# One decoder layer on one core: TensorE for the conditioning rows, tokens on partitions in the tail, other places for small loads

## The reference, cut to what matters

```python
c_act = silu(c)
sh1, sc1, gt1, sh2, sc2, gt2 = split(c_act @ ada_w + ada_b, 6)
h = rmsnorm(x, norm_mix_g) * (1 + sc1) + sh1
x = x + gt1 * hybrid_mixer(h)             # mixer ends in y @ w_out
h = rmsnorm(x, norm_ffn_g) * (1 + sc2) + sh2
logits = h @ router_w + router_b          # top 4 of 32, softmax over the 4
x = x + gt2 * moe(h, logits)              # act(h @ w1[e] + b1[e]) @ w2[e] + b2[e]
out = rmsnorm(x, final_norm_g)
```

## Time and profile before

| | us |
|---|---|
| median of three executions | 1461.37 (1460.83 to 1462.33) |
| the profiled execution | 1460.91 |
| its span, first to last instruction | 1459.1 |
| mean granted TensorE clock, share of full | 0.971 |

### The profile page before, as it was taken

How to read it: one execution, slowest core, us unless ns; L and a number is a source line. 1 busy time by engine, 2 the same in 40 slices (tenths; PEclk the granted TensorE clock), 3 DMA queues, 4 the chain that set the end, 5 groups by cost and what they waited for, 6 DMA issues and landing times.

```text
span 1459.1 us, 17602 instructions
## 1 busy us (share of the span) xinstructions
PE 1324.6 (91%) x6612; PEld 674.9 (46%) x6613; DVE 426.0 (29%) x1020; ACT 175.1 (12%) x355; POOL 73.8 (5%) x67
## 2 busy tenths in 40 slices
PE   1799998898998799999999999999999999989996
PEld 1688866878887433333322333233333233323332
DVE  5588625454312421121112111121211121112112
ACT  1000111121200211011001100010110010001102
POOL 1010003324100000000000000000000000000000
PEclk8799989999999799999999999999999999999999
DMA  9968551010434099999999999969999999999995
GB/s 319 387 235 299 192 200 59 0 59 1 141 144 155 27 429 426 426 425 428 427 425 425 428 427 427 424 266 425 428 427 426 425 428 426 427 425 425 429 426 217
DMA packets 68390, 471.79 MB, mean 323 GB/s; under 512 B 3965, under 2 KB 4154, under 8 KB 35466
## 3 DMA queue, kind: packets, MB, share of 16 engines
q1 hardware_dynamic: 67328, 468.89, 78.2%
q0 software_dynamic: 560, 1.40, 0.5%
q10 hardware_dynamic: 474, 1.11, 0.2%
HBM read 470.33 MB, written 1.05 MB: 323 GB/s over the span
## 4 chain that ended last, share of the span: by engine, by line
PE 53%; DMA 40%; DVE 5%; ACT 1%; issue 1%; ACTq 0%; SPq 0%; DVEq 0%
DMA ring<-in_exp_w_dram 39%; PE bank L683 18%; PE bank L1045 16%; PE bank L1071 5%; PE bank L1016 2%; PE bank L888 2%; PE bank L1083 1%; PE bank L885 1%; PE bank L878 1%; DVE region_z L1186 1%; PE bank L1037 1%; PE bank L801 1%; PE bank L705 1%; DMA ring<-in_ada_w_dram 1%; DMA work<-in_gdn_norm_g_dram 1%
## 5 line engine op out<-in xcount | busy, mean ns | idle before, releaser
L1045 PE MATMUL bank<-ring,work 128*64 128x512 f32 x2112 | 472.3, 598 | 48.8 <-DMA ring<-in_exp_w_dram 48.7
L1045 PEld LDWEIGHTS bank<-ring,work 128*64 128x64 f32 x2112 | 144.9, 137 | 372.5 <-issue 272.8
L1071 PE MATMUL bank<-ring,work 128*64 128x512 f32 x1056 | 233.9, 595 | 0.0
L683 PE MATMUL bank<-region_h,ring 128*128 128x256 f32 x832 | 187.4, 387 | 5.8 <-DVE region_h L1203 4.2
L683 PEld LDWEIGHTS bank<-region_h,ring 128*128 128x128 f32 x832 | 160.0, 194 | 29.4 <-DVE region_h L1203 4.3
L1071 PEld LDWEIGHTS bank<-ring,work 128*64 128x64 f32 x1056 | 72.9, 137 | 137.4 <-issue 137.4
L1515 DVE TENSOR_SCALAR work<-bank 128x256 f32<-128x256 f32 x66 | 27.6, 419 | 347.8 <-PE bank L1045 347.8
L642 ACT ACTIVATE work<-work 128x256 f32<-128x256 f32 x66 | 27.5, 416 | 765.2 <-DVE work L1515 765.2
L1542 DVE TENSOR_TENSOR work<-bank,work 128x512 f32<-128x512 f32 x33 | 22.8, 692 | 315.7 <-PE bank L1071 315.7
L1016 PE MATMUL bank<-qkv,work 128*64 128x512 f32 x272 | 65.7, 604 | 2.1 <-ACT qkv L618 2.1
L1083 PE MATMUL bank<-work 64*128 64x512 f32 x264 | 65.6, 615 | 0.8 <-DVE work L1542 0.8
(11 more groups left out here) (269 smaller groups left out, 958.4 us busy)
## 6 DMA issues: line engine op xcount, KB each, us to landing
ring<-in_exp_w_dram SPq DMA_DIRECT2D x192, 2048.0 KB, 23.7
ring<-in_w_in_dram SPq DMA_DIRECT2D x13, 2048.0 KB, 12.0
ring<-in_ada_w_dram SPq DMA_DIRECT2D x12, 2048.0 KB, 12.9
ring<-in_w_gdn_out_dram SPq DMA_DIRECT2D x2, 2048.0 KB, 7.8
ring<-in_w_out_dram SPq DMA_DIRECT2D x2, 2048.0 KB, 7.9
ring<-in_w_pool_out_dram SPq DMA_DIRECT2D x1, 2048.0 KB, 8.9
consts<-in_const_dram SPq DMA_DIRECT2D x1, 1153.0 KB, 6.4
region_x<-in_x_dram SPq DMA_DIRECT2D x2, 512.0 KB, 11.0
```

The source lines that it names most:

```text
L683: mm = nc.tensor.matmul(out_ap, w(k) if w else w_slot(n, j, k), rhs[:, k, :], start=(k == 0), stop=(k == kc - 1))
L1045: mm = nc.tensor.matmul(bank[b][h * SLOTS:(h + 1) * SLOTS, :], xT[:, c % 4, c // 4, :], slot_as(q, 2)[:, i, lo:lo + 512], start=False, sto ...
L1071: mm = nc.tensor.matmul(bank[2][o * SLOTS:(o + 1) * SLOTS, :], actT[:, b, c, h, :], slot_as(4 + b, 2)[:, h, lo:lo + 512], start=(b + h + c ...
```

## The change

**Start.** The `ada` chunks are cut by rows, two 128-row parts of all 2048 columns each. `ada_rows` multiplies them on PE: a column of `c_act`, spread over 32 columns, is stationary, and 512 columns of weights stream; four such calls go to four 32-partition strips of bank 5. ACT copies the bank to `ada_row`, four small matmuls bring it onto partitions (bank 4), and DVE adds the bias. `c` is turned by itself, the constants are loaded in two parts, SP waits for no rows, `hT` signals after each block, and the first projection waits block by block. POOL's small loads wait for `vec_hT`.

**Middle.** After the z pairs, PE computes sh2 @ router_w (g = 0), and spreads gt1 over partitions (g = 1, ACT copies it to `gt1_row`). DVE folds scale2 into `rw` and the product into `rb`.

**Tail.** w_out is streamed against stationary tokens (`mix_out`), so the result has tokens on partitions. DVE multiplies by `gt1_row` and adds x, per 512 columns. The raw x is turned and scored, the norm's factor is applied to the logits, and `h2` is made by DVE (scale) and POOL or DVE (shift) from spread rows. The two halves of the tokens run one behind the other. The mask comes from one comparison for all four ranks and one sum. The expert biases and `final_norm_g` are loaded by SP. Buffers move: the routing tables `b8` to `region_z`, others as named.

```diff
-        chunks = [("ada", cut(ada_w, CW * i)) for i in range(4)]
+        chunks = [("ada", ada_w[0, 2 * P * q:2 * P * (q + 1), 0:2 * D].rearrange("(c p) n -> p c n", p=P))
+                  for q in range(4)]
...
-            sp.dma_start(rows[ROW_C:ROW_C + 8, :], c.rearrange("b (r n) -> (b r) n", n=P)).then_inc(rows_in, 16)
-            sp.dma_start(rows[ROW_ADA_B:ROW_ADA_B + 48, :],
-                         ada_b.rearrange("l (r n) -> (l r) n", n=P)).then_inc(rows_in, 16)
-            sp.dma_start(consts[:, :], const).then_inc(const_in, 16)
+            sp.dma_start(rows[ROW_C:ROW_C + 8, :], c.rearrange("b (r n) -> (b r) n", n=P)).then_inc(c_in, 16)
+            sp.dma_start(consts[:, 0:2 * P], const[:, 0:2 * P]).then_inc(const_in, 16)
             for t in range(T):
                 sp.dma_start(xt[:, t, :], x[0, t * P:(t + 1) * P, :]).then_inc(x_in, 16)
-            sp.wait_ge(rows_in, 16 * 10)
             for n, (kind, src) in enumerate(chunks):
...
+                    dst = slot_as(n % RING, parts_of[kind])
                 sp.dma_start(dst, src).then_inc(landed[n % RING], 16)
+                if n == RING - 1:
+                    sp.dma_start(consts[:, 2 * P:CONST_W], const[:, 2 * P:CONST_W]).then_inc(tables_in, 16)
...
+            sp.wait_ge(vec_x1, 4)
+            for i in range(2):
+                at = slice(i * SLOTS, i * SLOTS + E)
+                sp.dma_start(b1_rows[at, :], exp_b1[0][:, i * D:(i + 1) * D]).then_inc(b_in, 16)
+                sp.dma_start(b2_rows[at, :], exp_b2[0][:, i * 512:(i + 1) * 512]).then_inc(b_in, 16)
+            sp.dma_start(fin_g, final_norm_g.partition_broadcast(P)).then_inc(fin_in, 16)
             sp.wait_ge(vec_route, 1)
...
+            pool.wait_ge(vec_hT, 1)
             pool.dma_start(pw, pool_w[0].rearrange("g p n -> p g n")).then_inc(early_in, 16)
...
+            pool.wait_ge(act_spread, 4)
+            pool.wait_ge(vec_h2, 1)
+            nc.gpsimd.tensor_tensor(h2[:, 0, :], h2[:, 0, :], shift_row, ALU.add).then_inc(pool_h2, 1)
...
-            act.wait_ge(vec_cols, 1)
-            nc.scalar.activation(c_act[:, :], cols[:, ROW_C:ROW_C + 8], ACT.Silu).then_inc(act_c, 1)
+            act.wait_ge(pe_c, 1)
+            nc.scalar.activation(c_act[:, :], bank[7][:, 0:8], ACT.Silu).then_inc(act_c, 1)
...
+            act.wait_ge(used[3], 1)
+            nc.scalar.activation(ada_row, bank[5][:, :], ACT.Copy).then_inc(act_adarow, 1)
...
+                if g:
+                    for i in range(2):
+                        act.wait_ge(pe_gt1, i + 1)
+                        nc.scalar.activation(gt1_row[:, i * 512:(i + 1) * 512], bank[6][:, :],
+                                             ACT.Copy).then_inc(act_gt1, 1)
...
+            for i, row in enumerate((scale_row, shift_row)):
+                act.wait_ge(pe_spread, i + 1)
+                for h in range(2):
...
+                    nc.scalar.activation(row.rearrange("q (c p) -> q p c", c=KC)[:, at, :],
+                                         bank[4 + 2 * i + h][:, :].rearrange("q (p c) -> q p c", c=KC),
+                                         ACT.Copy).then_inc(act_spread, 1)
...
+                    if each:
+                        pe.wait_ge(each, k + 1)
...
+            def ada_rows(q):
+
+                arrived(q)
+                w = slot_as(q % RING, 2)
+                for i in range(2):
+                    for j in range(4):
+                        mm = nc.tensor.matmul(bank[5][32 * j:32 * j + 32, :],
+                                              c_act[:, 2 * q + i:2 * q + i + 1].to_broadcast([P, 32]),
+                                              w[:, i, CW * j:CW * (j + 1)],
+                                              start=(q + i == 0), stop=(q == 3 and i == 1))
+                mm.then_inc(used[q % RING], 1)
+
             pe.wait_ge(const_in, 16)
-            pe.wait_ge(rows_in, 16 * 10)
+            pe.wait_ge(c_in, 16)
+            nc.tensor.transpose(bank[7][:, 0:8], rows[ROW_C:ROW_C + 8, :], ident[0:8, 0:8]).then_inc(pe_c, 1)
+            pe.wait_ge(act_c, 1)
+            ada_rows(0)
+            pe.wait_ge(vec_xn, 2)
+            for f in range(KC):
+                for t in range(T):
+                    mm = nc.tensor.transpose(turned(f)[:, t * P:(t + 1) * P], xt[:, t, f * P:(f + 1) * P], ident)
+            mm.then_inc(pe_xT, 1)
+            ada_rows(1)
+            ada_rows(2)
+            pe.wait_ge(rows_in, 16 * 9)
...
+            ada_rows(3)
+            pe.wait_ge(act_adarow, 1)
+            for i in range(4):
+                mm = nc.tensor.matmul(bank[4][:, 4 * i:4 * i + 4], ada_row[:, i * P:(i + 1) * P],
+                                      ident.rearrange("p (j a) -> p a j", j=4)[:, 0, :], start=True, stop=True)
+            mm.then_inc(pe_adacol, 1)
...
+
+            def spread(cols_, half, b):
+
+                for j in range(4):
+                    f = 4 * half + j
+                    mm = nc.tensor.matmul(bank[b][:, j * P:(j + 1) * P], cols_[:, f:f + 1].to_broadcast([P, P]), ident,
+                                          start=True, stop=True)
+                return mm
...
+                if g == 0:
+                    for k in range(KC):
+                        mm = nc.tensor.matmul(bank[6][:, 0:E], mod[:, 24 + k:25 + k].to_broadcast([P, P]), rw[:, k, :],
+                                              start=(k == 0), stop=(k == KC - 1))
+                    mm.then_inc(pe_rbias, 1)
+                else:
+                    pe.wait_ge(vec_rbias, 1)
+                    for i in range(2):
+                        if i:
+                            pe.wait_ge(act_gt1, 1)
+                        spread(mod[:, 16:24], i, 6).then_inc(pe_gt1, 1)
...
+            spread(scale2[:, :], 0, 4)
+            spread(scale2[:, :], 1, 5).then_inc(pe_spread, 1)
             pe.wait_ge(vec_yg, 4)
             for i in range(4):
                 n = chunk_no["gdn_out"][i // 2]
                 arrived(n)
                 tail_pair(i, n, i, region_z)
             pe.wait_ge(act_gate1, 4)
+            spread(mod[:, 24:32], 0, 6)
+            spread(mod[:, 24:32], 1, 7).then_inc(pe_spread, 1)
...
+            def mix_out(n, lo=0, hi=KC):
+
+                t, h = n // 2, n % 2
+                for k in range(lo, hi):
+                    mm = nc.tensor.matmul(bank[4 + n][:, :], region_y[:, k, t * P:(t + 1) * P],
+                                          ring[:, chunk_no["w_out"][h] % RING, k, :],
+                                          start=(k == 0), stop=(k == KC - 1))
+                    if n == 0 and k == 0:
+                        carry(mm)
+                if hi == KC:
+                    mm.then_inc(pe_mo, 1)
...
+            def turn_x1(n):
+                t, h = n // 2, n % 2
+                pe.wait_ge(vec_x1, n + 1)
+                for j in range(4):
+                    f = 4 * h + j
+                    mm = nc.tensor.transpose(bank[n][:, j * P:(j + 1) * P], xt[:, t, f * P:(f + 1) * P], ident)
...
+            def score(t):
+                for k in range(KC):
+                    mm = nc.tensor.matmul(bank[4 + t][:, 0:E], x1T[:, k, t * P:(t + 1) * P], rw[:, k, :],
...
+            mix_out(0)
+            mix_out(1)
+            turn_x1(0)
+            pe.wait_ge(act_spread, 4)
+            mix_out(2)
+            free_slot(chunk_no["w_out"][0])
+            turn_x1(1)
+            mix_out(3, 0, 4)
+            turn_x1(2)
+            pe.wait_ge(act_x1T, 2)
+            score(0)
+            mix_out(3, 4, KC)
+            free_slot(chunk_no["w_out"][1])
+            for j in range(4):
+                for h in range(2):
+                    f = 4 * h + j
+                    mm = nc.tensor.matmul(bank[6][h * SLOTS:(h + 1) * SLOTS, j * P:(j + 1) * P],
+                                          mod[:, 40 + f:41 + f].to_broadcast([P, SLOTS]), ident, start=True, stop=True)
+                    if f == 0:
+                        carry(mm)
             mm.then_inc(pe_gt2, 1)
...
-            pe.wait_ge(act_h2, 4)
+            pe.wait_ge(pool_h2, 1)
...
+            dve.wait_ge(pe_adacol, 1)
+            link(tt(mod[:, 0:16].rearrange("p (j i) -> p i j", j=4),
+                    bank[4][:, 0:16].rearrange("p (i j) -> p i j", i=4),
+                    cols[:, ROW_ADA_B:ROW_ADA_B + 16].rearrange("p (j i) -> p i j", j=4), ALU.add))
             link(stt(scale1[:, :], mod[:, 8:16], 1.0, cols[:, ROW_G1:ROW_G1 + 8], ALU.add, ALU.mult))
             dve.wait_ge(pe_xT, 1)
             for f in range(KC):
...
+                if g == 0:
+                    dve.wait_ge(pe_rbias, 1)
+                    tt(rb[:, :], rb[:, :], bank[6][:, 0:E], ALU.add)
+                    for k in range(KC):
+                        ins = ts(rw[:, k, :], rw[:, k, :], scale2[:, k:k + 1], None, ALU.mult)
+                    ins.then_inc(vec_rbias, 1)
...
+            def add_mixed(n):
+                dve.wait_ge(pe_mo, n + 1)
```

(58 more changed lines are left out.)

244 lines of the change are left out of this document (92 added, 152 removed).

## The result

The kernel after takes **1436.30 us** (median of four executions, 1435.84 to 1441.35), the one before 1461.80 in four: 25.5 us less. Forecast were 1437.0 and 1428 to 1447. The profiled execution took 1435.84, span 1434.0, granted clock 0.979.

What follows compares the result with a forecast made beforehand. The expert stage was taken as a byte-bound weight stream, so only its beginning, set by the block table, counts. Start -15.1, middle +4.7, tail -13.8 sum to -24.2 on 1460.91: 1436.7, plus 0.46 for the median, 1437; range 1428 to 1447.

Steps and rivals of the forecast that it cites:

- three stages: Parts of the chain ahead of the expert stream: start -15.1 us, middle +4.7, tail -13.8.
- Start: Up to the first projection: it begins at 33.3 instead of 48.36, with PE at half clock, -15.1 us.
- full clock: Rival in the start: the light load keeps PE at 1.00, -4.4 us more, up to -7; 1431, chance 0.15.
- ring late: Rival: after the start the second `qkv` chunk comes 1 to 6 us late and everything shifts; 1441, chance 0.15.
- Four strips at once: In `ada_rows`: four calls to different strips run together, 1.76 us at full clock against 7.04 one by one.
- two-strip row: Earlier profile row the strips estimate rests on: 32 passes of 512 columns in 7.02 us, a full factor of two.
- The small loads: POOL's six loads moved behind `vec_hT`: users past 138 us; 0.47 MB priced at 3.8 us in a rival.
- Middle: Passes put ahead of the L864 transposes delay the path in full, 1.9 and 2.8 us: +4.7, up to 8.
- Ahead of w_out: Tail around w_gdn_out: filled gap and full clock -1.7, passes behind it +0.4; w_out starts at -1.3 us.
- w_out to gather(0): Tail from w_out's start to the gather: 42.2 us instead of 54.7, -12.5.
- Gather to table: Tail's end, from gather to block table: 11.8 us stay; a full clock would give back up to 3.4.
- Stream: Expert stage: the weight stream's length is unchanged, 31 experts at 29.5 us; late biases would delay bias(0) one for one.

Runs made afterwards that it cites:

- strips_apart: The kernel after with the two loops of `ada_rows` exchanged, so a strip's two calls follow each other: 1438.87 us, ratio 0.984.
- strip_one: The kernel after with all four calls of `ada` chunks 1 to 3 sent to one strip, sums not the reference's: 1430.38 us, ratio 0.9782.
- small_early: The kernel after without POOL's wait for `vec_hT`, so its small loads go out at the start as before: 1441.98 us, ratio 0.9863.
- gap_open: The kernel after with the spread of scale2 moved from ahead of w_gdn_out to behind it: 1440.35 us, ratio 0.9853.
- table_first: The kernel after with the block table's two transposes moved ahead of bias(0): 1435.25 us, ratio 0.9816.
- combo_later: The kernel with mid_moved, warm, table_first and tables_late together, plus POOL's small loads behind the first silu: 1426.65 us, ratio 0.9757.
- mid_moved: The kernel after with the router's product (g = 0) and gt1's spread (g = 1) issued behind the turns: 1432.36 us, ratio 0.9802.
- mask_old: The kernel after with the mask made by a loop over the ranks, as before: 1438.03 us, ratio 0.9833.
- tables_late: The kernel after with the second part of the constants (1.02 MB) loaded three chunks later: 1436.02 us, ratio 0.9824.
- warm: The kernel after with nine idle-time identity matmuls, read by nobody, added ahead of gather(0): 1433.36 us, ratio 0.9802.
- start_only: The kernel before with only the start of the change, middle and tail as before: 1448.96 us, ratio 0.9912.

## Why the prediction was right

It was right in the time and in the three stages, each within 2.2 us; inside the stages errors cancel.

- **Start, -15.1 forecast, -15.3 in the profile.** The last `ada` chunk was used at 27.36, not 26.2; 1.0 us of this stands at the first chunk already (12.54 against 11.5). It then took 1.92 at full clock, not 3.5 at half, and the small product 1.06, not 1.87. The first block of `hT` was under way at 31.59, and PE waited for the first `qkv` chunk until 32.78, where it was due at 31.6. The second chunk was late too, 1.33 us, where the prediction had 1.4 us of slack. The rival "full clock" and the rival "ring late" both came true in part and cancelled, so that the start's number is partly luck. The clock there is not settled by the code: of ten profiles with this start (without strips_apart, strip_one and small_early), the last chunk took 1.92 us in four (after, gap_open, table_first, combo_later) and 2.7 to 3.6 in six. In each of the four PE then waited some 1.7 us for the first `qkv` chunk, in none of the six; the first projection starts at 32.9 on average in the four and at 34.0 in the six, so a full clock there gives back about 1 us.
- **Four strips at once.** Shown by strip_one: 1.92 against 6.96, where the prediction reckoned 1.76 and 7.04 at full clock. The two-strip row was a sound guide. The Trainium skill gives up to 4x ("TensorEngine Tiling (Array Packing)", Theoretical Speedup), with which this agrees, and 2.38x measured for three column strips ("TensorE: Matmul & The Clock Gate", Measured speedup vs the span model); the 3.6x of four here speak against carrying the latter over.
- **The small loads.** The prediction gave their users and their 3.8 us as a rival's price, and no term of their own. They cost 5.3 us where they stood (small_early). The place past the `ada` chunks is what counts, not that they are late for anything.
- **Middle, +4.7 forecast, +3.9.** 1.73 and 2.16; mid_moved gives all of it back by place alone. The first was right; in the second the wait for ACT was 0.69 and the passes 1.05 and 1.16.
- **Ahead of w_out, -1.3 forecast, -1.6.** gap_open shows both parts: the filled gap and the clock of the next product.
- **w_out to gather(0), 42.2 forecast, 40.0.** The four turns of x were taken at 0.98 each and cost 0.60 to 0.66 (1.5 of the 2.2 us). That was a miscount: in the earlier trace rows L962 is 16 transposes and stands as x16, so a transpose counts once where a product counts twice, and a turn of four is 0.49 by that row.
- **Gather to table, unchanged forecast, +2.1.** This step failed, though small. The turns back into `h2`, which kept PE busy there before, are gone, and PE ran at 0.51 from 462 to 479. But the stretch varies: with the same instructions it took 13.4 to 14.0 us in six profiles (13.92 in after), 11.86 in mask_old and 10.36 in tables_late. warm shows that work in the idle time brings the gather to full clock, 1.7 us of it. That the change itself makes the slow form likelier is only argued: of before's form there are two profiles, 11.8 and 11.7 in start_only.
- **Stream.** Unchanged, as forecast, and the biases were not late.

Open: why the start ends up to 3 us apart between profiles of the same code, and why the rate columns have two forms 1.7 us apart. The clock of the last `ada` chunk and the times at which x and the chunks land go with the first, but no experiment holds one of them fixed.

## What to carry to other kernels

In a kernel that ends in a stream at the memory's pace, the only thing to price is the moment at which the stream begins; price it stage by stage along PE, and ask at each added pass whether PE idles just behind it, for then its place costs more than its work. Look for small loads of another queue beside the first large ones: a wait of one line was worth some 5 us here. And when a wait is taken away, name the next one first (here the ring's slot behind the block table).

## What was not expected

- Eight calls of 32 stationary columns each, spread over four strips, take their 16 passes in 1.92 us, 0.12 a pass, 3.6 times as fast as into one, and the order of the loops makes no difference (1.94).
- Behind heavier work the clock stayed up: with all calls in one strip PE ran its 48 passes at full clock, and the 127 passes behind them took 27.73, against 15.49 for the first 64 (14.08 for the next) in after.
- Nine matmuls of the identity that nobody reads took the gather from 3.68 to 1.94 us; the median of the kernel is 2.9 us lower with them.
- The same 96 passes at the rate columns take 19.3 us in half of the profiles and 21.0 in the others, also where the code up to there is the same.
- Without the one expert that has a second block the kernel is 12.8 us shorter behind the table (strip_one).
